# Fetching the gate operands of the joining stage from ScalarE's queue

## The reference

```
for x in (gla, gdn):
    o   = forward[x] + backward[x]                      # (1024, 1024)
    o   = o * rsqrt(mean(o*o, over each head) + 1e-6) * norm_w[x]
    y_x = o * silu(g[x]) * sigmoid(r[x])                # g, r: gates, made by earlier matmuls
mix = y_gla + y_gdn                                     # then mix @ w_out
```

## Time and profile before

| | us |
|---|---|
| median of 3 runs | 5377.94 |
| lowest and highest of them | 5344.79, 5491.37 |
| the profiled execution, its own time | 5307.42 |
| its span | 5305.6 |
| the joining stage, from its first large load to its last VectorE instruction | 4289.4 to 4500.4 |

### The profile page before, as it was taken

One profiled execution on the slowest core, in us unless ns is written; L12 is line 12 of the kernel. 1 busy time (PEld: TensorE's weight loads), 2 busy tenths in 40 slices (PEclk: granted clock), 3 DMA queues, 4 the chain that ended last, 5 costly groups with the idle time before them and its releaser, 6 DMA issues. The chain is left out here.

```text
span 5305.6 us, 63105 instructions
## 1 busy us (share of the span) xinstructions
PE 3798.9 (72%) x24826; PEld 2922.7 (55%) x24826; DVE 1967.5 (37%) x2433; ACT 1065.0 (20%) x1560; POOL 898.1 (17%) x626
## 2 busy tenths in 40 slices
PE   3797884838769997468997886495399920748992
PEld 1796444837535554357996764242388820636661
DVE  5213446061446664231105552423344457221112
ACT  0111222110313332110111223312123232101121
POOL 0001230000234442000002100000244434011002
PEclk7898885959879998789998997698699965859996
DMA  6322003232642211332212222454544333249984
GB/s 235 102 73 76 6 20 118 79 133 74 222 92 60 60 38 72 135 115 84 96 61 91 67 68 72 124 124 129 180 116 119 99 137 147 106 147 367 323 293 174
DMA packets 392620, 641.09 MB, mean 121 GB/s; under 512 B 97437, under 2 KB 253725, under 8 KB 387933
## 3 DMA queue, kind: packets, MB, share of 16 engines
q1 hardware_dynamic: 373978, 587.47, 34.3%
q10 hardware_dynamic: 10880, 25.17, 1.6%
q0 software_dynamic: 7568, 25.70, 1.3%
HBM read 451.17 MB, written 187.09 MB: 120 GB/s over the span
## 5 line engine op out<-in xcount | busy, mean ns | idle before, releaser
L455 PE MATMUL in_ps_p<-in_wh,h 128*128 128x352 f32 (+1 forms) x1600 | 363.1, 314 | 21.5 <-DVE in_wl L468 21.5
L455 PE MATMUL out_ps_p<-out_wh,m 128*128 128x256 f32 (+1 forms) x1152 | 279.8, 336 | 54.2 <-DVE out_wl L468 54.2
L455 PEld LDWEIGHTS in_ps_p<-in_wh,h 128*128 128x128 f32 x1600 | 273.4, 191 | 22.3 <-DVE in_wl L468 12.7
L455 PE MATMUL rest__ps_p<-rest__wh,h 128*128 128x388 f32 x1024 | 265.5, 340 | 15.5 <-DVE rest__wl L468 15.5
L1822 PE MATMUL cg_ps_p<-h,cg_wh 128*128 128x512 f32 x768 | 247.5, 404 | 14.2 <-POOL cg_wl L1801 14.2
L1594 PE MATMUL la_ps_s<-la_q,la_k 104*128 104x512 f32 x960 | 254.1, 400 | 2.5 <-DVE la_q L1674 2.5
L3213 PE MATMUL ex_ps_g<-ex_wgu,ex_xt 128*128 128x256 f32 x1024 | 234.7, 388 | 27.0 <-ACT ex_xt L3247 13.3
L455 PE MATMUL in_ps_p<-in_wl,h 128*128 128x352 f32 (+1 forms) x800 | 250.9, 314 | 0.0
L1632 ACT ACTIVATE la_pt<-la_ps_s 128x1024 f32<-128x1024 f32 x160 | 163.7, 1023 | 399.8 <-PE la_ps_s L1594 399.8
L455 PEld LDWEIGHTS out_ps_p<-out_wh,m 128*128 128x128 f32 x1152 | 200.6, 194 | 76.7 <-issue 46.5
L1549 POOL TENSOR_TENSOR la_accp<-la_accp,la_pt 128x1024 f32<-128x1024 f32 x80 | 195.0, 2438 | 229.4 <-ACT la_pt L1632 229.4
(11 more groups left out here) (580 smaller groups left out, 7574.5 us busy)
## 6 DMA issues: line engine op xcount, KB each, us to landing
ex_wgu<-in_moe_w_gate_dram SPq DMA_DIRECT2D x32, 1024.0 KB, 8.2
ex_wgu<-in_moe_w_up_dram SPq DMA_DIRECT2D x32, 1024.0 KB, 10.7
ex_wd<-in_moe_w_down_dram SPq DMA_DIRECT2D x32, 1024.0 KB, 9.7
ada_w<-in_w_ada_dram SPq DMA_DIRECT2D x12, 2048.0 KB, 18.1
dl_row<-rows SPq DMA_DIRECT2D x32, 512.0 KB, 4.7
yb<-ex_y SPq DMA_DIRECT2D x32, 512.0 KB, 6.3
p<-in_o SPq DMA_DIRECT2D x8, 1760.0 KB, 7.2
rest__w<-in_w_in_dram SPq DMA_DIRECT2D x16, 776.0 KB, 8.1
```

Source lines behind the costliest of these rows:

```text
L455: mm = te.matmul(ps[n % NB][:, 0:cw], a, b, start=k == 0 and n_ == 0, stop=k == kt - 1 and n_ == 2)
```

## The change

The loads of r and m leave SP's stream. They are issued on ACT's queue, at the head of each round and ahead of the round's squares, job by job, each pair behind a wait for the step that read the buffer last in the round before (`g00` and so on, the product on VectorE). SP keeps the loads of f and b, with its waits as they were.

```diff
--- before.py
+++ after.py
@@ -2861,8 +2861,6 @@
                         sp.wait_ge(*(dve.before(it, f"add{s}") if x else pe.before(it, f"tr{s}")))
                         sp.dma_start(f[j][:], (gla, gdn)[x][0][rows, :]).then_inc(fb_in[j].sem, 16)
                         sp.dma_start(b[j][:], (gla, gdn)[x][1][rows, :]).then_inc(fb_in[j].sem, 16)
-                        sp.dma_start(r[j][:], p2g[x][rows, :]).then_inc(g_in[j].sem, 16)
-                        sp.dma_start(m[j][:], p2r[x][rows, :]).then_inc(g_in[j].sem, 16)
 
             @block.gpsimd
             def _(gp):
@@ -2882,6 +2880,12 @@
             def _(act):
                 act_s.open(act)
                 with act.Fori(0, rounds) as it:
+                    for s, x in jobs:
+                        j = (s, x)
+                        rows = place(act, (it * 2 + s) * P, P)
+                        act.wait_ge(*dve.before(it, f"g{s}{x}"))
+                        act.dma_start(r[j][:], p2g[x][rows, :]).then_inc(g_in[j].sem, 16)
+                        act.dma_start(m[j][:], p2r[x][rows, :]).then_inc(g_in[j].sem, 16)
                     for s, x in jobs:
                         act.wait_ge(*pool.now(it, f"ad{s}{x}"))
                         act.wait_ge(*(dve.now(it, f"sm0{x}") if s else dve.before(it, f"sm1{x}")))
```

## The result

The changed kernel takes 5469.68 us (median of 4 runs, 5465.9 to 5476.7), the kernel before 5361.43 (4 runs, 5344.79 to 5491.37). Without the run at 5491, which is in the slower of the two states of this kernel, the ratio of the mean times is 1.0214, 95% interval 1.0167 to 1.0261. By the medians that is 108 us more where I forecast 13 less, and outside my range. The changed kernel's profiled execution took 5467.67 us, 160 more than that of before, 5307.42.

The account below looks back on a forecast made before the run. In the joining stage, serial loading then work was taken as the bound, no engine being full. Rounds 1 to 3 at -5 us each plus 2 for round 0 gave -13: 5294.4 us by profile, 5365 by median, range 5310 to 5425.

Parts of the forecast that it names:

- How the numbers follow: Whole kernel: case chances and range, from 5365 with -25 and +27 around no change, plus 35 us scatter each side.
- The chances: Whole kernel's time: faster by over 2% 0.02, within 2% 0.95, slower 0.03.
- None comes near 106 us: Whole kernel: no forecast case or rival reaches 106 us, which is 2% of the time.
- Part 1: Joining stage, rounds 1 to 3: gates issued earlier off SP's queue save 5 us a round, bounds 3 and 6.
- Part 2: Joining stage, round 0: two evenly sharing queues land the last b later, +2 us, bounds -1 and +2.4.
- Parts 3 to 5: ACT's eight issues a round, SP's shorter stream, extra waits and registers: nothing each; SP's stream bounds 0 and -0.5 a round.
- Sum, -13: All parts together: -15 us from rounds 1 to 3 plus 2 from round 0, bounds -21 and -6.6.
- slower: mixing two queues lowers the rate: Stage's loads: DMA rate drops from 410 to 250 GB/s with both queues, +27 us in all; chance 0.10.
- Nothing gained: Stage's loads: a second issuer brings no bytes and the early start is given back, -6 to +3 us; chance 0.20.
- more gained: Stage's loads: f and b on SP's queue overtake the gates, at most -38 us, 5340 by the median; chance 0.10.

Follow-up runs that it names:

- three pairs: Changed kernel against the kernel before, without dense matmuls, with twelve, with 24: stage 202.6 against 211.6, 201.3 against 210.5, 202.3 against 210.9 us.
- the kernel with only the waits: Kernel before plus only the change's four gate waits on ScalarE, all loads still on SyncE: 5487.4 us profiled, twelve runs 5306.7 to 5489.6.

## Why the prediction was wrong

- The step that failed is one in "How the numbers follow", "a scatter of a median of three of some 35 us to each side". I took the spread from 5307 to 5491 for scatter around one middle and put the centre at the median of three. It is two levels 160 us apart, a loop at one of two clocks, and a median of few runs is a draw from them. The changed kernel's first four runs all had the high level, at 30 in 70 for one of the kernel before a chance of 0.43 to the fourth, 3%, if the edit has no part in it. So the measured sign is that of the loop's level, and not that of the edited stage. With its six later runs it stands at 6 of 10 at that level. Its cause was to be suspected in the one trace I had: the clock goes from 0.50 to 1.00 as the loop starts, and I looked at no stage but the edited one.
- The chances (0.95 within 2%) failed by the same step. The range doesn't come out of its own working either: no change is 5378, and 25 and 27 around it with 35 more to each side give 5318 to 5440, not 5310 to 5425. 5469.68 is outside both. "None comes near 106 us" is right for the stage and wrong for the kernel.
- Part 1, 5 us a round: the last sum behind SP's first issue came 4.0, 2.9 and 3.7 us sooner, around the low end of my 3 to 6. The mechanism held, its size was 3.5 us a round instead of 5. Where I had the last b 17.3 us behind the first f, the last sum starts 18.2 to 19.0 us behind it. In round 1 the start is not what is missing: 350 GB/s in the first 5 us behind SP's issue and then 409 to 420, with 1.8 MB sent ahead of it, put the end of all bytes at the full rate at 4532.8, 16.9 us behind the first f. But the rate falls off before the end, to 250 and 29 GB/s in two successive microseconds, and the last sum starts at 4534.03, 1.2 us behind that point, where I had allowed half a microsecond.

```profile
4509.00:4516.00 7.00, 1.96 (x8) 1.57 (x8) 6.93 (x6) 0.00 (x0) 2.24 (x1) 0.50 0.77 257
4516.00:4521.00 5.00, 1.96 (x8) 1.57 (x8) 4.71 (x5) 0.00 (x0) 0.00 (x0) 0.50 1.00 350
4521.00:4526.00 5.00, 0.00 (x0) 0.00 (x0) 1.12 (x1) 0.00 (x0) 0.34 (x1) 0.50 1.03 420
4532.00:4533.00 1.00, 0.00 (x0) 0.00 (x0) 1.00 (x1) 0.50 (x1) 1.00 (x1) 0.50 0.63 250
4533.00:4534.00 1.00, 0.00 (x0) 0.00 (x0) 1.00 (x2) 0.00 (x0) 0.89 (x1) 0.50 0.07 29
```

- Part 2, round 0, +2 with bounds -1 and +2.4: 53.1 against 51.8 us, +1.3. Right.
- Parts 3 to 5, nothing each: ACT is done with its issues 1 us behind SP's first f, and ACT's wait at the round's start grew to 27 to 29 us. Right.
- Sum, -13: the stage gave -9.0, -9.2 and -8.6 in three pairs, the time with the loop's clock lifted -17 and -12. The direction was right, the size of the stage within my bounds of -7 to -21.
- The rivals: "slower: mixing two queues lowers the rate" is out, 409 to 420 GB/s with both queues. "Nothing gained" is out. The idea behind "more gained" was right in that f and b ahead of the gates are worth much more (33 us of stage), only the edit doesn't do it: the queues share evenly.

The Trainium skill's rule that I weighed ("DMA: Bandwidth & Descriptors", "Issuing engines are not separate DMA queues") holds: the second queue brought no bytes, and without an earlier start it cost 5 us.

What stays open: whether the edit shifts the odds of the loop's clock without dense matmuls (6 of 10 runs at the upper level against 30 of 70 can't tell, but only 1 of 10 is at the lower one against 31 of 70, which equal odds would give in some 4% of cases; the kernel with only the waits has 3 of 12 there); what the runs between the levels are (5372 to 5446), for which no profile was taken: their mean clock lies between as well, which fits a clock that rises in mid-loop, but that is a guess; why 7 of the 58 runs with 24 dense matmuls still lie above 5400, at a mean clock of 0.808 to 0.818; what the two runs at 6110 and 6140 are, with 0.669 and 0.666; and what the dense matmuls themselves cost, as the medians with 24 (5317.7 and 5310.7 of the changed kernel) and with 12 (5295.6) are from different chips.

## What to carry to other kernels

When two kernels differ, set the traces side by side by stage before explaining anything by the edit; here the profiles were 160 us apart, and a loop that nobody had touched was 173.6 longer, against 9 the other way in the edited stage. A loop of thin matmuls that can hold either clock makes the kernel's time a draw of two levels; put dense work ahead of it before you measure an edit worth less than the distance, and look at the single runs, not at a median of three. In the edited stage, order loads by what is waited for first, and release each buffer by its own last reader: that was worth 40 us where a second queue was worth 9.

## What the runs showed of the hardware

- A loop in which PE is busy 147.8 of 150 us at 1.2 GHz stayed there for 408 us; the same loop at 2.4 GHz, with PE busy 139.9 of 150 us, stayed there too. In the two profiles it was settled in the loop's first 20 us. The Trainium skill, "TensorE: Matmul & The Clock Gate", Part 1, says that the low clock is the default and activity releases it, and that how many matmuls run at the low clock differs between runs. The traces agree that the low clock comes first (0.50 ahead of the loop in both) and that the number of matmuls at it differs between executions. That activity releases it they show in one; in the other PE was busy 147.8 of 150 us and the clock was not released before the loop ended.
- Twelve or 24 dense 128x128 by 512 matmuls ahead of it left 68 of 79 runs, of all kernels with them, at the lower level of time, against 31 of 70 of the kernel before without.
- Two hardware queues with 512 KB loads share the engines evenly: with f and b on one and the gates on the other the sums came 5.1 us apart at 412 to 417 GB/s in all, twice the 2.56 us that a job's two loads would need alone at 410 GB/s (an estimate from their 1.05 MB).
